# Expert weights fetched as 16 KB runs into eight rotating slots, with permuted features, in a two-block transformer kernel

## The chip, the cores and the metric

The kernel runs on one core of a Trainium2 chip. The metric is the device time in microseconds (us) of one execution; lower is better.

## The reference, cut to what matters

The reference is a transformer: a first block (attention and a gated recurrence, then a layer of 16 experts), two further blocks with dense feed-forward layers, and a final norm. All tensors are float32, 256 tokens of 1,024 features. The change lies in the layer of experts, in which each expert takes the 32 tokens (`cap`) that like it most:

```python
def expert_choice_moe(h, w_router, w_gate, w_up, w_down):
    B, S, D = h.shape                                   # 1, 256, 1024
    cap = max(1, CAPACITY_FACTOR * S // N_EXPERTS)      # 32
    logits = jnp.einsum('bsd,de->bse', h, w_router).astype(jnp.float32)
    aff = jax.nn.softmax(logits, axis=-1)
    gate, idx = lax.top_k(aff.transpose(0, 2, 1), cap)
    xin = jax.vmap(lambda hb, ib: hb[ib])(h, idx)
    hid = jax.nn.silu(jnp.einsum('becd,edf->becf', xin, w_gate)) * jnp.einsum('becd,edf->becf', xin, w_up)
    y = jnp.einsum('becf,efd->becd', hid, w_down) * gate[..., None].astype(h.dtype)
    return jnp.zeros_like(h).at[bidx, idx].add(y)
```

Each of the 16 experts has three matrices of 1,024 x 1,024 float32, 4 MiB each, so the layer reads 201.3 MB. Every weight is used once.

## The kernel before

The program is one block with a stream for each engine, ordered by semaphores. The queue of SP issues all weight loads. ACT and DVE take results out of PSUM, and PE has eight PSUM banks (`bank(b)`, 512 float32 in each partition). Banks 0 to 3 hold the residual sum for the whole layer of experts; banks 4 to 7 are for the experts' own products.

**Loads.** `half` (L426 to L430) fetches 512 columns of all 1,024 rows of one matrix, 2 MiB. Row k*128+p goes to partition p, so a partition gets eight runs of 2 KB (512 float32). There are six places in `ring` (`slot(0)` to `slot(5)`: the two column halves of gate, of up and of down) and two more in `odd_slot`, which take the first halves of gate and of up for every other expert. `loads` waits on the semaphores `used0`, `used1` and `used2` (products of gate, up and down done) and issues the next loads in a fixed order. For the first expert two halves of gate are fetched early, half of up when the first block's weights are done with, and five more halves after `acc_done`.

**PE, one expert** (`expert`, in a loop of eight turns with two experts each):

1. `gather` (L800): 16 products of the normed tokens `xn` with a one-hot matrix `hot_next` put this expert's tokens, features on partitions, into bank 4. DVE scales them by the norm's weight into `xin` (L1686).
2. `quarter` (L811), four times: gate columns 0 to 511 into bank 4, up columns 0 to 511 into bank 5, then the other halves into the same two banks. A quarter has eight products with 32 stationary columns; four of them (`j`) write four groups of 32 partitions of the bank at once, and each group sums a part of the features. Since both halves use one bank, a second half waits until the first has been copied out (`g4_done`, `u4_done`).
3. Two transposes (L829) of `hot_e`, the one-hot matrix weighted by the affinity, for the way back.
4. Fold (L844): 16 products with `fold` add the four partition groups and put hidden features on partitions, into banks 6 and 7 (gate and up of a column half in one bank). ACT applies silu (L1210) and DVE multiplies (L1702), half by half, into `hidT`. PE waits for both halves.
5. Two quarters for down (L811) into banks 5 and 4, copied out by DVE and ACT (L1705, L1212).
6. Four products (L854) with `back` add the result to banks 0 to 3. The last of them count `half_done` and `stage_done`; when these have counted all 16 experts the dense layers start with the update and norm of ACT and DVE.

A product is shown in the trace as two MATMUL records (float32 goes through PE in two passes), so a quarter is x16.

**After the experts.** The memory of `ring` is used again: `raw_sb`, `wh_sb`, `wl_sb`, `xTh_sb`, `xTl_sb`, `hidh_sb` and `hidl_sb` lie in it, in this order. The first weights of the dense layers are fetched once `used0` says that the last expert's gate is done (POOL passes this on as `raw_free`).

Of the kernel before, what the change touches and what calls it, by code (L numbers as in the profile page):

```python
# [15 lines left out]
P = 128  # L16
# [123 lines left out]
def two_blocks(nc, x_in, w_in, w_out, wg, wu, wd, relb, f1g, f1u, f1d, w_in2, w_out2, f2g, f2u, f2d,  # L140
               const, band, onehot, future, one, prm_in, fin_w, out):
    with ExitStack() as ctx:
# [45 lines left out]
        def slot(s, n=512):  # L188
            return ring[:, s * SLOT:s * SLOT + KD * n].rearrange("p (k n) -> p k n", k=KD)

# [16 lines left out]
        n_ss, n_eps, n_std, n_rstd, hold = st(3), st(1), st(TT), st(TT), st(6)  # L207
# [46 lines left out]
        hot = t2(TT * (NE + 1) * CAP).rearrange("p (t e c) -> p t e c", t=TT, e=NE + 1)  # L254
# [5 lines left out]
        affT, topw, chosen, place, ones_e = [t2(S)[0:NE, :] for _ in range(5)]  # L260
# [8 lines left out]
        odd_slot = [t2(SLOT).rearrange("p (k n) -> p k n", k=KD) for _ in range(2)]  # L269
# [55 lines left out]
        def pf(name, i=None):  # L325
# [4 lines left out]
        names = """x_in0 x_in1 const_in one_in band_in mask_in w1_in0 w1_in1 w1_hi w1_lo ex_in0 ex_in1 ex_in2 ex_in3 ex_in4 ex_in5 odd_in0 odd_in1  # L330
            mxT_ps k_scaled late_in tb_out tb_in raw_in0 raw_in1 raw_in2 fin_out
            half_done sq_done ss_ready std_ready rstd_ready diag_dve diag_act xn_dve xn_act xnT_ps xT_act xT_dve acc_done x_act x_dve
            z_ready z_hq z_hf z_hb z_q z_k z_v z_hi z_hg
            lb_max lb_exp lb_done gate_sg gate_lf lev_sub lev_exp lev_q lev_k lev_ps lev_put
            qk_sq qk_ms qk_std qkT_ps qT_done kT_done
            sc_ps sc_nm sc_exp sc_cnt eT_ps eT_act eT_dve o_ps o_put ho_ps ho_sq ho_ms ho_std ho_put gs_done
            masks_zero lg_ps lg_nm lg_exp aff_done affT_ps place_done placeT_ps hot_done xin_ps
            xe_ready hote_done used0 used1 used2 back_ps g4_done u4_done back_done sum_ps esil_done ehid_done
# [8 lines left out]
        ex_in = [sem["ex_in0"], sem["ex_in1"], sem["ex_in2"], sem["ex_in3"], sem["ex_in4"], sem["ex_in5"]]  # L347
# [8 lines left out]
        def buf(f, r):  # L356
            return RUNS["ffn", f, r][0]
# [14 lines left out]
        def used_ffn(L, f, r, s):  # L372

            return used[buf(f, r)], 2 * NE + PRODUCTS[buf(f, r)] * L + RUNS["ffn", f, r][2] + s + 1

        def used_mix(L, m):

            return used[buf_mix(m)], 2 * NE + PRODUCTS[buf_mix(m)] * L + RUNS["mix", m][2] + 1
# [19 lines left out]
        def _(sp):  # L398
# [6 lines left out]
            for p in range(W1):  # L405
# [26 lines left out]
            def first_half(row, odd):  # L432
                half(row, wg, 0, odd_slot[0] if odd else slot(0), sem["odd_in0"] if odd else ex_in[0])
                half(row, wu, 0, odd_slot[1] if odd else slot(2), sem["odd_in1"] if odd else ex_in[2])

            REST = [(1, wg, 1), (3, wu, 1), (5, wd, 1), (4, wd, 0)]
# [3 lines left out]
            half(0, wg, 0, slot(0), ex_in[0])  # L440
            sp.wait_ge(sem["lev_put"], NLEV + 1)
            half(0, wg, 1, slot(1), ex_in[1])
# [8 lines left out]
            half(0, wu, 0, slot(2), ex_in[2])  # L451
            sp.wait_ge(sem["acc_done"], 1)
            for i, w, c in REST[1:]:
                half(0, w, c, slot(i), ex_in[i])
            first_half(D, True)
# [3 lines left out]
            def loads(e, j, downs_last=True):  # L459

                def value(v):
                    return v if isinstance(v, int) else sp.snap(v)

                half_free, free = value(2 * e + 1), value(2 * e + 2)
                row, row_next = value(D * e + D), value(D * e + 2 * D)

# [4 lines left out]
                for r, w in enumerate((wg, wu)):  # L472
                    if downs_last:
                        next_half(r, w)
# [1554 lines left out]
```

## Time and profile before

| | |
|---|---|
| device time, median of 3 runs | 1729.85 us (1727.73 to 1731.01) |
| profiled execution, its span | 1726.3 us |
| PE matmul busy | 1606.1 us, 93% |
| DVE busy, ACT busy | 750.1 us, 663.7 us |
| moved by DMA | 400.12 MB |
| experts, first product to last | 238.8 to 729.5 us |

The profiled execution's own time is its span, 1726.3 us, and what lies before the first and behind the last instruction; the median of the runs shown is 3.5 us above the span. In the profile, PEclk is the granted clock of TensorE as a share of 2.4 GHz (0.5 is 1.2 GHz), DMA is the busy share of the 16 DMA engines, and an arrow (`<-`) names what an engine waited for. PE records are pipelined, so their durations overlap slightly.

### The profile page before, as it was taken

Reading aid. Unit: us, or ns where it says so; the run is one execution under the profiler, and the core shown is the slowest. Engines: PE = TensorE matmul, PEld = TensorE weight load, DVE = VectorE, ACT = ScalarE, POOL = GpSimd, SP = SyncE. Lnnn points to the kernel's source line nnn. Section 1 sums busy time; section 2 is a strip of 40 time slices with the busy share of each in tenths; the row PEclk is TensorE's granted clock in tenths of the full one; section 3 lists DMA queues with packets and bytes.
Section 4 is the critical chain, followed back from the end, with each engine's and each line's share of the span. In section 5 each row is a group of like instructions: output and inputs, shape, how many; then the busy total and the mean of one; then the engine's idle time right before and its main releaser. Section 6 shows DMA issues by size and latency. Waiting matters only on the chain.

```text
span 1726.3 us, 26493 instructions
## 1 busy us (share of the span) xinstructions
PE 1606.1 (93%) x10974; PEld 1299.6 (75%) x10974; DVE 750.1 (43%) x1004; ACT 663.7 (38%) x757; POOL 46.6 (3%) x34
## 2 busy tenths in 40 slices
PE   7996878897888888999999999999999999999998
PEld 7885744443443444499999979999999999889997
DVE  4679531110101101164445765444554447754444
ACT  5564322111111111354345554433634354753343
POOL 0015200000000000000000000000000000000000
PEclk9898979788778878999999999999999999999999
DMA  7522599999999999965555535555465555346552
GB/s 241 178 80 73 198 339 386 387 387 387 387 387 387 387 387 387 369 220 179 185 191 158 163 98 196 193 178 163 152 215 191 174 170 182 115 138 202 193 181 86
DMA packets 249052, 400.12 MB, mean 232 GB/s; under 512 B 4720, under 2 KB 135200, under 8 KB 248864
## 3 DMA queue, kind: packets, MB, share of 16 engines
q1 hardware_dynamic: 247808, 397.74, 66.8%
q10 hardware_dynamic: 1184, 1.57, 0.3%
q8 instruction: 39, 0.64, 0.2%
q14 instruction: 21, 0.17, 0.0%
HBM read 398.23 MB, written 1.06 MB: 231 GB/s over the span
## 4 chain that ended last, share of the span: by engine, by line
PE 65%; SPq 20%; DVE 5%; DMA 4%; issue 3%; ACT 3%; POOL 0%; ACTq 0%; DVEq 0%; POOLq 0%
SPq L430 20%; PE ps L581 12%; PE ps L583 12%; PE ps L582 12%; PE ps L606 6%; PE ps L607 6%; PE ps L608 6%; PE ps L811 4%; DMA ring<-w_in 2%; PE ps L552 2%; PE ps L543 1%; PE ps L800 1%; DMA ring<-w_expert_down 1%; PE ps L844 1%; PE ps L854 1%
## 5 line engine op out<-in xcount | busy, mean ns | idle before, releaser
L1715 DVE TENSOR_TENSOR wl_sb<-raw_sb,wh_sb 128x2048 fp32r<-128x2048 f32 x162 | 370.8, 2292 | 294.1 <-ACT wh_sb L1220 293.8
L581 PE MATMUL ps<-xTh_sb,wh_sb 128*128 128x256 f32 x1696 | 482.2, 284 | 1.0 <-DVE xTl_sb L1410 1.0
L583 PE MATMUL ps<-xTh_sb,wl_sb 128*128 128x256 f32 x1696 | 479.9, 283 | 0.0
L582 PE MATMUL ps<-xTl_sb,wh_sb 128*128 128x256 f32 x1696 | 479.9, 283 | 0.0
L1220 ACT ACTIVATE wh_sb<-raw_sb 128x2048 fp32r<-128x2048 f32 x162 | 309.8, 1915 | 300.0 <-PE ps L583 186.4
L581 PEld LDWEIGHTS ps<-xTh_sb,wh_sb 128*128 128x128 f32 x1696 | 325.3, 192 | 4.5 <-DVE xTl_sb L1410 2.5
L582 PEld LDWEIGHTS ps<-xTl_sb,wh_sb 128*128 128x128 f32 x1696 | 325.4, 192 | 2.2 <-issue 0.7
L583 PEld LDWEIGHTS ps<-xTh_sb,wl_sb 128*128 128x128 f32 x1696 | 325.4, 192 | 0.0
L811 PE MATMUL ps<-ring,work 128*32 128x512 f32 x1280 | 206.0, 791 | 60.8 <-DMA ring<-w_expert_up 38.9
L811 PEld LDWEIGHTS ps<-ring,work 128*32 128x32 f32 x1280 | 45.7, 136 | 182.6 <-issue 153.1
L606 PE MATMUL ps<-wh_sb,hidh_sb 128*128 128x512 f32 x384 | 151.2, 394 | 1.2 <-DVE wl_sb L1715 1.2
L607 PE MATMUL ps<-wl_sb,hidh_sb 128*128 128x512 f32 x384 | 149.9, 390 | 0.0
L608 PE MATMUL ps<-wh_sb,hidl_sb 128*128 128x512 f32 x384 | 149.5, 389 | 0.0
L1698 DVE COPY work<-ps 128x512 f32<-128x512 f32 x32 | 22.1, 692 | 180.5 <-PE ps L811 180.5
L1231 ACT ACTIVATE work<-ps 128x512 f32<-128x512 f32 x44 | 26.5, 603 | 164.0 <-PE ps L583 164.0
L844 PEld LDWEIGHTS ps<-const_sb,work 128*128 128x128 f32 x512 | 70.2, 224 | 19.4 <-issue 19.4
L606 PEld LDWEIGHTS ps<-wh_sb,hidh_sb 128*128 128x128 f32 x384 | 72.3, 188 | 16.2 <-DVE wl_sb L1715 2.0
L608 PEld LDWEIGHTS ps<-wh_sb,hidl_sb 128*128 128x128 f32 x384 | 72.1, 188 | 15.4
L607 PEld LDWEIGHTS ps<-wl_sb,hidh_sb 128*128 128x128 f32 x384 | 72.3, 188 | 13.8 <-issue 0.5
L844 PE MATMUL ps<-const_sb,work 128*128 128x32 f32 x512 | 72.1, 305 | 0.0
L1727 DVE SCALAR_TENSOR_TENSOR work<-work,ps 128x512 f32<-128x512 f32 x44 | 30.4, 690 | 94.0 <-ACT work L1231 94.0
L800 PEld LDWEIGHTS ps<-work,xn_sb 128*128 128x128 f32 x512 | 63.7, 203 | 8.6 <-issue 7.2
(294 smaller groups left out, 1775.2 us busy)
## 6 DMA issues: line engine op xcount, KB each, us to landing
ring<-w_expert_down SPq DMA_DIRECT2D x32, 2048.0 KB, 19.7
ring<-w_expert_gate SPq DMA_DIRECT2D x24, 2048.0 KB, 19.4
ring<-w_expert_up SPq DMA_DIRECT2D x24, 2048.0 KB, 19.8
raw_sb<-ffn_gate SPq DMA_DIRECT2D x44, 1024.0 KB, 5.4
raw_sb<-ffn_up SPq DMA_DIRECT2D x44, 1024.0 KB, 5.3
raw_sb<-ffn_down SPq DMA_DIRECT2D x44, 1024.0 KB, 4.9
raw_sb<-w_in SPq DMA_DIRECT2D x22, 1024.0 KB, 5.4
ring<-w_in SPq DMA_DIRECT2D x16, 1024.0 KB, 5.6
```

What stands on the lines that cost most here:

```text
L430: sp.dma_start(to, rows.rearrange("(k p) n -> p k n", p=P)).then_inc(landed, 16)
L581: pe.matmul(to, w_h[:, k, fs], x_h[:, k, :], start=k == 0, stop=False)
L582: pe.matmul(to, w_h[:, k, fs], x_l[:, k, :], start=False, stop=False)
L583: mm = pe.matmul(to, w_l[:, k, fs], x_h[:, k, :], start=False, stop=k == KD - 1)
L606: pe.matmul(to, left_h[:, k, ts], w_h[:, k, ns], start=False, stop=False, skip_group_check=True)
L607: pe.matmul(to, left_h[:, k, ts], w_l[:, k, ns], start=False, stop=False, skip_group_check=True)
L608: mm = pe.matmul(to, left_l[:, k, ts], w_h[:, k, ns], start=False, stop=last and k == 1, skip_group_check=True)
L800: mm = pe.matmul(bank(4)[:, k * CAP:k * CAP + CAP], xn[:, t, k * P:k * P + P], hot_next[:, t, :], start=t == 0, stop=t == TT - 1)
L811: mm = pe.matmul(bank(b)[j * CAP:j * CAP + CAP, :], stationary[:, Q4 * r + j, :], w[:, Q4 * r + j, :], start=r == 0, stop=r == KD // Q4 - ...
L844: mm = pe.matmul(bank(6 + c)[:, a:a + CAP], src[:, f * P:f * P + P], fold, start=True, stop=True)
L1220: nc.scalar.activation(wh[j], raw[j], ACT.Copy).then_inc(sem["w_hi"], 1)
L1715: dve.tensor_tensor(wl[j], raw[j], wh[j].bitcast(F32), ALU.subtract).then_inc(raw_free[j], 1)
```

## The change

It does five things.

- **Runs.** `half` now takes rows instead of columns: partition p gets rows 8p to 8p+7 of the matrix, of which a half is four whole rows, one run of 16 KB in memory. A partition thus holds features 8p+k and not k*128+p.
- **Features permuted.** To match, `xn` is written permuted (ACT and DVE, `permuted`), the norm's weight is loaded a second time in that order (`norm2p`, a small DMA in the first phase), and `g4` and `u4` are written by ACT and DVE with the features in the order k, q (`"p q k"` read, `"p k q"` written), so that the fold gives hidden features in the order in which down's rows lie.
- **Slots.** Eight slots in rotation: load q (six for each expert) goes to slot q % 8, as soon as the counter `half_used` says that product q-8 is done.
- **Banks.** A half has all 1,024 columns for half of the features, so a matrix's product is two half products, each into two banks: gate and down in banks 4 and 5, up in 6 and 7. `n0_ps` tells that the first bank of the two is complete.
- **Order.** The next expert's gather stands between the fold of gate and that of up. The transposes stand first in an expert, and the back products wait for both copies of the result. PE's loop has four turns with four experts each. Silu is one instruction.

The diff at its core (arguments, names of semaphores and what follows from them left out):

```diff
-        g4, u4, y4 = [[t2(512) for _ in range(2)] for _ in range(3)]
-        e_sil = [t2(4 * CAP) for _ in range(2)]
+        g4, u4 = [t2(FE).rearrange("p (k q) -> p k q", k=KD) for _ in range(2)]
+        y4 = [t2(512) for _ in range(2)]
+        e_sil = t2(KD * CAP)
...
+        slots = [ring[:, s * SLOT:s * SLOT + SLOT] for s in range(6)] + [t2(SLOT) for _ in range(2)]
+        NS = len(slots)
+        def expert_rows(s):
+            return slots[s].rearrange("p (j n) -> p j n", j=Q4)
+        def permuted(a):
+            return a.rearrange("p (k q) -> p q k", k=KD)
...
+                    sp.dma_start(norm2p, bass.AP(one.tensor, a, [[1, KD], [KD * ONE_N, P // KD], [ONE_N, KD]]),
+                                 allow_slow_non_contiguous=True).then_inc(sem["mask_in"], 16)
...
-            def half(row, w, c, to, landed):
-                rows = w.rearrange("e d f -> (e d) f")[bass.ds(row, D), 512 * c:512 * c + 512]
-                sp.dma_start(to, rows.rearrange("(k p) n -> p k n", p=P)).then_inc(landed, 16)
+            def half(i, row, s):
+                rows = (wg, wu, wd)[i // 2].rearrange("e d f -> (e d) f")[bass.ds(row, D), :]
+                lines = rows.rearrange("(p k) n -> p (k n)", p=P)
+                sp.dma_start(slots[s], lines[:, (i % 2) * rows_of:(i % 2 + 1) * rows_of]).then_inc(ex_in[s], 16)
...
+            for i in range(3, 6):
+                half(i, 0, i)
+            for i in range(2):
+                half(i, D, 6 + i)
...
+            def next_half(q, taken, row):
+                sp.wait_ge(sem["half_used"], taken)
+                half(q % 6, row, q % NS)
+            TURN = 4 * 6
+            with sp.Fori(0, (NE * 6 - NS) // TURN) as g:
+                for j in range(TURN):
+                    next_half(NS + j, sp.snap(TURN * g + j + 1), sp.snap(4 * D * g + D * ((NS + j) // 6)))
...
+            def product(b, stationary, q, landed):
+                h, w = q % 2, expert_rows(q % NS)
+                pe.wait_ge(ex_in[q % NS], landed)
+                for n in range(2):
+                    for j in range(Q4):
+                        mm = pe.matmul(bank(b + n)[j * CAP:j * CAP + CAP, :], stationary[:, Q4 * h + j, :],
+                                       w[:, j, 512 * n:512 * n + 512], start=h == 0, stop=h == 1, skip_group_check=True)
+                    if h == 1 and n == 0:
+                        mm.then_inc(sem["n0_ps"], 1)
+                mm.then_inc(sem["half_used"], 1)
...
+                pe.wait_ge(sem["hote_done"], e_th(1, 1))
+                for t in range(TT):
+                    mm = pe.transpose(bank(UP_PS + 1)[:, t * P:t * P + P], hot_e[:, t, :, :].rearrange("p j c -> p (j c)"), ident)
+                mm.then_inc(sem["back_ps"], 1)
+                pe.wait_ge(sem["xe_ready"], e_th(1, 1))
+                product(GATE_PS, xin, q, landed(q))
+                product(GATE_PS, xin, q + 1, landed(q + 1))
+                pe.wait_ge(sem["back_done"], e_th(1, 1))
+                product(UP_PS, xin, q + 2, landed(q + 2))
+                product(UP_PS, xin, q + 3, landed(q + 3))
+                pe.wait_ge(sem["g4_done"], e_th(2, 2))
+                fold_up(g4, GATE_PS, range(KD)).then_inc(sem["fold_ps"], 1)
+                pe.wait_ge(sem["hot_done"], e_th(1, 2))
+                pe.wait_ge(sem["u4_done"], e_th(2, 1))
+                gather()
+                pe.wait_ge(sem["u4_done"], e_th(2, 2))
+                fold_up(u4, GATE_PS + 1, range(Q4)).then_inc(sem["fold_ps"], 1)
+                fold_up(u4, UP_PS + 1, range(Q4, KD)).then_inc(sem["fold_ps"], 1)
+                pe.wait_ge(sem["ehid_done"], e_th(2, 1))
+                product(GATE_PS, hidT, q + 4, landed(q + 4))
+                pe.wait_ge(sem["ehid_done"], e_th(2, 2))
+                product(GATE_PS, hidT, q + 5, landed(q + 5))
+                pe.wait_ge(sem["y4_act"], e_th(1, 1))
+                pe.wait_ge(sem["y4_dve"], e_th(1, 1))
...
-            with pe.Fori(0, NE // 2) as i:
-                expert(i, 0)
-                expert(i, 1)
+            pe.wait_ge(sem["hot_done"], 1)
+            gather()
+            with pe.Fori(0, NE // 4) as g:
+                for i in range(4):
+                    expert(g, i)
...
+                for n in range(2):
+                    act.wait_ge(*((sem["half_used"], 6 * e + 2) if n else (sem["n0_ps"], 3 * e + 1)))
+                    nc.scalar.activation(g4[:, :, 64 * n:64 * n + 64].rearrange("p k q -> p q k"),
+                                         bank(4 + n).rearrange("p (q k) -> p q k", k=KD), ACT.Copy).then_inc(sem["g4_done"], 1)
+                act.wait_ge(sem["fold_ps"], 3 * e + 1)
+                nc.scalar.activation(e_sil, bank(4)[:, 0:KD * CAP], ACT.Silu).then_inc(sem["esil_done"], 1)
...
+            dve.wait_ge(sem["xin_ps"], 1)
+            next_tokens()
+            next_hot(1)
             with dve.Fori(0, NE) as e:
...
+                for n in range(2):
+                    dve.wait_ge(*((sem["half_used"], 6 * e + 4) if n else (sem["n0_ps"], 3 * e + 2)))
+                    dve.tensor_copy(u4[:, :, 64 * n:64 * n + 64].rearrange("p k q -> p q k"),
+                                    bank(6 + n).rearrange("p (q k) -> p q k", k=KD)).then_inc(sem["u4_done"], 1)
+                dve.wait_ge(sem["xin_ps"], e + 2)
+                next_tokens()
+                next_hot(e + 2)
```

## Rows read from the trace of the kernel before

**Rows 1.** The page: the span, PE's clock and DMA in 40 slices.

```profile
span 1726.3 us, 26493 instructions
...
PEclk9898979788778878999999999999999999999999
DMA  7522599999999999965555535555465555346552
GB/s 241 178 80 73 198 339 386 387 387 387 387 387 387 387 387 387 369 220 179 185 191 158 163 98 196 193 178 163 152 215 191 174 170 182 115 138 202 193 181 86
```

**Rows 2.** Windows: us, busy time of each engine, PEclk, DMA share, GB/s.

```profile
300.00:650.00 350.00, 297.52 (x1817) 146.73 (x1817) 37.75 (x95) 55.40 (x84) 0.00 (x0) 0.80 1.05 387
715.00:720.00 5.00, 4.97 (x44) 3.78 (x36) 1.08 (x3) 1.80 (x3) 0.00 (x0) 1.00 1.05 387
720.00:725.00 5.00, 4.34 (x28) 1.09 (x32) 1.01 (x3) 0.28 (x1) 0.00 (x0) 0.66 1.07 365
```

**Rows 3.** Waits of PE from 300 to 650: us in total, times, longest.

```profile
PE ps L811 <- DMA ring<-w_expert_up: 37.0, 11, 4.9
PE ps L811 <- DVE work L1702: 7.6, 11, 0.7
PE ps L811 <- DVE work L1686: 5.6, 10, 0.6
PE ps L811 <- DMA ring<-w_expert_down: 4.6, 3, 2.5
```

**Rows 4.** Timeline of PE, the last expert (no wait for DMA).

```profile
704.54 3.65 PE L800 MATMUL ps<-work,xn_sb 128*128 128x32 f32 x32
708.71 3.64 PE L811 MATMUL ps<-work 128*32 128x512 f32 x32 [0.52 <-DVE work L1686]
712.28 0.44 PE L829 MATMUL ps<-const_sb,work 128*128 128x128 f32 x2
712.64 3.64 PE L811 MATMUL ps<-ring,work 128*32 128x512 f32 x32
716.22 3.76 PE L844 MATMUL ps<-const_sb,work 128*128 128x32 f32 x32
720.66 5.25 PE L811 MATMUL ps<-ring,work 128*32 128x512 f32 x32 [0.69 <-DVE work L1702]
725.85 3.70 PE L854 MATMUL ps<-work 128*128 128x512 f32 x8
```

**Rows 5.** Timeline of PE, groups that ran at the lower clock.

```profile
231.17 7.03 PE L800 MATMUL ps<-work,xn_sb 128*128 128x32 f32 x32 [1.32 <-DVE work L1672]
238.80 5.54 PE L811 MATMUL ps<-ring,work 128*32 128x512 f32 x32 [0.61 <-DVE work L1686]
...
333.60 3.64 PE L811 MATMUL ps<-ring,work 128*32 128x512 f32 x16 [4.67 <-DMA ring<-w_expert_up]
337.17 7.04 PE L844 MATMUL ps<-const_sb,work 128*128 128x32 f32 x32
```

**Rows 6.** Windows, as rows 2, while a load with 12 KB runs is moved.

```profile
25.50:29.00 3.50, 3.50 (x32) 3.50 (x32) 0.00 (x1) 1.96 (x2) 0.00 (x0) 1.00 1.06 440
26.00:28.00 2.00, 2.00 (x19) 2.00 (x18) 0.00 (x0) 0.95 (x1) 0.00 (x0) 1.00 1.03 432
```

**Rows 7.** Timeline of SP's queue around the first expert.

```profile
211.27 3.73 SPq L430 DMA_DIRECT2D ring<-w_expert_down  x2
215.04 5.22 SPq L430 DMA_DIRECT2D work<-w_expert_gate  x1
220.30 5.66 SPq L430 DMA_DIRECT2D work<-w_expert_up  x1
230.82 0.30 SPq L457 DMA_DIRECT2D rel_bias_band<-work  x1
242.69 4.49 SPq L430 DMA_DIRECT2D ring<-w_expert_gate  x2
```

**Rows 8.** Groups by form from 400 to 595: count, busy us, mean ns, idle before.

```profile
L1698 DVE COPY work<-ps 128x512 f32<-128x512 f32 x12 | 8.3, 692 | 77.3 <-PE ps L811 77.3
L1203 ACT ACTIVATE work<-ps 128x512 f32<-128x512 f32 x6 | 3.6, 597 | 53.0 <-PE ps L811 53.0
L1693 DVE TENSOR_SCALAR work<-work 128x128 f32 x12 | 2.8, 279 | 0.0
```

**Rows 9.** Timeline of ACT in the first phase, two pieces of weights.

```profile
58.77 1.92 ACT L1080 ACTIVATE w1h_sb<-ring 128x2048 fp32r<-128x2048 f32 x1 [0.26 <-DMA ring<-w_in]
64.58 1.91 ACT L1080 ACTIVATE w1h_sb<-ring 128x2048 fp32r<-128x2048 f32 x1 [3.89 <-DMA ring<-w_in]
```

**Rows 10.** The page: the queue that fetches PE's code (packets, MB, share).

```profile
q8 instruction: 39, 0.64, 0.2%
```

More of the change, by code:

```diff
@@ L259, in two_blocks @@
         r_mx, r_nm, r_sum, r_rec = t2(TT), t2(TT), t2(TT), t2(TT)
-        affT, topw, chosen, place, ones_e = [t2(S)[0:NE, :] for _ in range(5)]
+        topw, chosen, place, ones_e = [t2(S)[0:NE, :] for _ in range(4)]
         top8 = t2(8)[0:NE, :]
@@ L450, in _ @@
             sp.wait_ge(sem["w1_lo"], W1)
[L451 removed]
+            half(2, 0, 2)
             sp.wait_ge(sem["acc_done"], 1)
[L453 to L455 removed]
+            for i in range(3, 6):
+                half(i, 0, i)
+            for i in range(2):
+                half(i, D, 6 + i)
             sp.wait_ge(sem["tb_rows_done"], 1)
             sp.dma_start(tb_dram.ap(), tb_rows).then_inc(sem["tb_out"], 16)
[L459 to L466, printed above, removed]
[L468 to L482 removed]
@@ L484, in _ @@
-            with sp.Fori(0, NE // 2 - 2) as i:
-                for j in range(2):
-                    loads(sp.snap(2 * i + j), j)
-            loads(NE - 4, 0)
-            loads(NE - 3, 1, downs_last=False)
-            for r, (i, w, c) in enumerate(REST):
-                if r < 3:
-                    sp.wait_ge(used[r], 2 * (NE - 1))
-                half(D * (NE - 1), w, c, slot(i), ex_in[i])
+            def next_half(q, taken, row):
+                sp.wait_ge(sem["half_used"], taken)
+                half(q % 6, row, q % NS)
@@ L799, in gather @@
                     for t in range(TT):
[L800 removed]
+                        mm = pe.matmul(bank(UP_PS)[:, k * CAP:k * CAP + CAP], xn[:, t, k * P:k * P + P], hot_next[:, t, :],
                                        start=t == 0, stop=t == TT - 1)
                 mm.then_inc(sem["xin_ps"], 1)
[L804 to L814 removed]
@@ new lines, in fold_up, with expert, value, landed @@
+            def fold_up(src, b, ks):
+                for i, k in enumerate(ks):
+                    mm = pe.matmul(bank(b)[:, i * CAP:i * CAP + CAP], src[:, k, :], fold, start=True, stop=True)
+                return mm
+            def expert(g, i):
+                def value(per, v):
+                    return pe.snap(per * g + v)
+                def landed(q):
+                    return value(16 * TURN // NS, 16 * (q // NS) + 16)
+                def e_th(per, v):
+                    return value(4 * per, per * i + v)
+                q = 6 * i
+                pe.wait_ge(sem["hote_done"], e_th(1, 1))
[12 more added lines that the diff above has]
+                pe.wait_ge(sem["u4_done"], e_th(2, 1))
+                gather()
+                pe.wait_ge(sem["u4_done"], e_th(2, 2))
[7 more added lines that the diff above has]
+                pe.wait_ge(sem["y4_dve"], e_th(1, 1))
+                for t in range(TT):
+                    for n in range(2):
@@ L1255, in _ @@
                 norm(3 * L + 2, pf("norm0"), XT1 + 14 * L,
-                     between=lambda: hi(buf(0, GATE), nth(L, 0, GATE, 0), (used[0], 2 * NE + PRODUCTS[0] * L)))
+                     between=lambda: hi(buf(0, GATE), nth(L, 0, GATE, 0), (used[0], 1 + PRODUCTS[0] * L)))
                 hi(buf(0, UP), nth(L, 0, UP, 0))
@@ L1957, in _ @@
             pool.memset(ones_e, 1.0).then_inc(sem["masks_zero"], 1)
-            pool.memset(hot[:, :, NE, :], 0.0).then_inc(sem["masks_zero"], 1)
-            pool.wait_ge(sem["used0"], 2 * NE)
+            pool.memset(hot[:, :, NE:NE + 2, :], 0.0).then_inc(sem["masks_zero"], 1)
+            pool.wait_ge(sem["half_used"], 6 * (NE - 1))
             for j in range(3):
                 pool.memset(hold[:, 1 + j:2 + j], 0.0).then_inc(raw_free[j], 1)
+            pool.wait_ge(sem["half_used"], 6 * (NE - 1) + 3)
+            for j in range(3):
+                pool.memset(hold[:, 6 + j:7 + j], 0.0).then_inc(used[j], 1)
             pool.wait_ge(sem["stage_done"], NE)
```

138 lines of the change are left out of this document (38 added, 100 removed).

## The prediction, written before the change was run

> **What bounds the kernel now.** I read the page's 40 slices first [rows 1]. DMA is at the top of its scale for ten slices, from about 259 us, at 387 GB/s, and PEclk is below 9 in most of these; behind them PE is the full engine and DMA is half busy. So the layer of experts is the one stretch that DMA could bound. The window 300 to 650 confirms it: DMA share 1.05 throughout, PE busy 297.5 of 350 us [rows 2]. The waits of PE there say which wait ends last: 41.6 us for expert weights and 13.2 us for two short DVE steps [rows 3]. In this state an expert takes 12.58 MB / 387 GB/s = 32.5 us. The timeline then gives what PE would need by itself: the last expert, with no wait for DMA, takes 704.54 to 729.55, 25.0 us [rows 4]. The whole layer, first product to last, is 238.8 [rows 5] to 729.55 [rows 4], 490.7 us, or 30.7 us an expert: below 32.5, because eight of the 96 halves are there before the first product. DMA is still full at 715 to 720 [rows 2], so the load stream and PE end together. What follows is PE's and is not touched; a gain at 729.55 passes through to the end.
>
> **The rate of DMA.** A half now is one run of 16 KB in each of 128 partitions instead of eight of 2 KB. The trace has no such runs. The nearest is a load in runs of 12 KB: 440 GB/s over 3.5 us and 432 GB/s over 2 us of it [rows 6]. Below, the bound is the rate of today, 387 [rows 2]. I take 430, close under the 12 KB rows, because short windows book a load's edges unevenly. A half of 2.097 MB then takes 4.88 us instead of 5.42, and 88 halves 429.4 us instead of 476.9.
>
> The Trainium skill (DMA: Bandwidth & Descriptors, Why small descriptors are slow) states a fixed overhead of about 3 cycles for each packet, beside one cycle for 32 bytes. By that, runs of 2 KB would lose 4% to it and long runs nearly nothing, so a rate of 1.04 x 387 = 403 GB/s and a stream shorter by 18 us instead of 47. The step from 387 to 440 in rows 2 and 6 is 1.14, so the trace speaks for the larger figure. The same page (Latency and other measured facts, HBM row pitch at large powers of two) speaks against such layouts: rows at pitches of some hundred KB and more in powers of two lost rate. Here partitions lie 32 KB apart, a power of two but well below, and no row of the trace shows such a loss.
>
> **When DMA's stream ends.** Before, the first load behind the prefetched eight is issued at 242.69 [rows 7], when the first product is done; that stream of 88 halves ends at about 242.7 + 1.4 + 476.9 = 721. After the change the first product starts later: DVE now makes the next one-hot matrix and both halves of `hot_e` (279 ns each, [rows 8]) and PE the transposes (0.44, [rows 4]) before it. That is 0.3 + 0.56 + 0.44 = 1.3 us. The five loads behind `acc_done` finish earlier and only lengthen the gap, since no slot is free. So the stream starts at 245.4 and ends at 674.8. Slots don't starve it: PE gives back four in its first 8 us, which keep DMA busy for 19.5 us, and the fifth about 18 us after the start. Behind the last load less is left than it seems: the last expert's fourth half lands at 665.0, then come its product (1.8), fold and gather (7.2 at the full clock), down (3.6), the copy (0.9) and the back products (3.7), 682.2; with the lower clock (next part) about 686.
>
> **When PE's work ends.** The number of products, their shapes and the weight loads are the same. I take the last expert's 25.0 us [rows 4] and change it:
>
> - Removed: the wait for `xin` (0.52) and that for `hidT` (0.69) [rows 4]. The first goes since the gather stands well ahead of its use; the second since the first half of `hidT` is made under the second half of up's fold, and the second under a product. The waits of a second half for the copy of the first go into other banks. 25.0 - 1.2 = 23.8.
> - Freed of the low clock: down took 5.25 where the same 32 records take 3.64 [rows 4]. 22.2 at the full clock.
> - Added: the back products wait for DVE's copy of bank 5, which starts only when the last product ends. 692 ns [rows 8] and two handovers, 0.9. 23.1. Before, DVE's copy lay under the other quarter and PE didn't wait.
> - The copies of gate and up write with a stride. They take 597 and 692 ns now [rows 8]; strided I allow up to twice that. Gate's lie under up's two products (3.64), up's under fold and gather (7.2): no cost. If they took over 3 us, PE would wait.
> - The clock. Fold and gather have 32 columns a product; after a fold and its wait down ran at the lower level (5.25, [rows 4]). Now fold and gather stand together: 64 records, 7.2 us. Below: one fall as today, 1.6. Above: both groups at the lower level (7.04 instead of 3.7, twice, [rows 4, 5]) and both down products too (3.64 for one, [rows 5], instead of 1.8): 6.7 + 3.6 = 10.3. I take one group at the lower level and one fall behind it, 3.3 + 1.7 = 5.0.
>
> So 28.1 us an expert (24.7 to 33.4). PE starts at 240.1, its first products run at the lower clock (5.54 against 3.64, [rows 5]) and 16 experts take 449.6: it ends at 240.1 + 1.9 + 449.6 = 691.6.
>
> **Sum.** DMA allows an end at 686, PE one at 691.6. The two are close, so in some experts PE will still find a half missing; I add 1.5 and expect the last back product at 693 instead of 729.55: 36.5 us earlier. Smaller terms: `norm2p` is 1,024 elements of 4 bytes in SP's queue, ahead of a piece of weights. ACT already waited 0.26 and 3.89 for such pieces [rows 9]; between 0 and 3 us, I take 0.5. The first dense weights may be fetched from the last expert's start and land at about 684, before they are used. Code: below. In total 36.0, on the profiled execution 1726.3 to 1690.3, and as the median of runs 3.5 above the span, 1694.
>
> **Rivals.**
>
> 1. DMA sets the end to the last: the clock falls once an expert as today, PE needs 24.7 and waits for weights. End 684 to 687, time about 1686. For it: waits for DMA dominate now [rows 3]. Against it: the longer run of narrow products. Chance 0.2.
> 2. The rate rises little or not: HBM or the pitch holds it. A quarter of the way from 387 to 440 [rows 2, 6], at 400 GB/s, a half takes 5.24 us, the stream ends at 706.7 and the layer, 11.4 later as above, at 718: time 1719. At 387 it is 722.3 + 11.4 = 733.7, time 1735. The page's rule of 3 cycles (403 GB/s) is this case and gives 1716. For it: no row has 16 KB runs. Against it: [rows 6]. Chance 0.11, of which 0.04 at no gain.
> 3. PE becomes the bound and it is slower than before (the other side). The clock stays low through fold, gather and down, at over 30.4 us an expert ((729.55 - 242.0) / 16 is 30.5) the layer is slower; at 31.5 the end is 746, time 1746. For it: the gather and the fold both took 7.04 at the lower level [rows 5], and PE idles between gate's and up's halves when it is ahead. Against it: a wait of 4.67 was followed by low products, but the loss was paid by time PE had anyway. Chance 0.09, 0.04 of it between 29.5 and 30.4, still faster.
> 4. PE's loop body doubles, from two experts to four, and the code has to be read again in every turn. Code was fetched in 39 packets over the whole run, 0.2% of the 16 engines' span, 1.4 us a packet [rows 10]. If half of that came again and nothing hid it, 20 packets cost 28 us: 1722. Halves that have landed meanwhile hide most of it, since PE then catches up. Chance 0.05. By the Trainium skill (Runtime: NRT & Kernel Launch, Instruction fetch mechanics) PE's instruction memory holds 2,048 instructions, so that such a body would fit; no run here shows its size.
>
> The forecast (PE and DMA close together, 1684 to 1708) has 0.55.
>
> **How the numbers follow.** About 0.2% (3.5 us) is what a measurement tells from no change. Faster: 0.55 + 0.2 + 0.07 (rival 2 at some gain) + 0.04 (rival 3) + 0.03 (rival 4) = 0.89. Same: 0.02. Slower: 0.04 + 0.05 = 0.09. For the range I reach from 1681 (rival 1 at 435 GB/s) to 1720, which takes in 400 GB/s and 29.8 us an expert. Left out: no gain in rate, the slow side of PE and of the code, and a little below.
>
> **What would show it.** In the window 300 to 650: GB/s about 430 at a full share if DMA is still the bound; below 425 with a share under 1.0 says that PE gives slots back too late. PE's waits for expert weights at L811's successor fall from 41.6 us; a wait of 0.7 to 1.0 for DVE's copy appears at each expert's back products. Fold and gather of one expert: 7.2 us says that the clock holds, over 10 that it doesn't. The copies of gate and up: 0.6 to 0.7 us each, or more by their stride. The last back product ends at 693. The prediction is wrong if the rate stays below 410, or if an expert takes PE more than 29.5 us.

## The result, and the profile after

The changed kernel takes 1688.13 us (median of 4 runs, 1686.92 to 1695.01) against 1730.43 us for the kernel before beside it: ratio 0.9771, 95% interval 0.9748 to 0.9794. Forecast were 1694 us and a range of 1681 to 1720. Run again later beside the experiments it took 1692.74 us, ratio 0.9787 (0.9767 to 0.9808).

The page of the changed kernel, the lines that answer to [rows 1]:

```profile
span 1686.5 us, 26658 instructions
...
PEclk9897977878787888999999999999999999999999
DMA  7632479999999999665555436564565546346552
GB/s 233 178 100 76 171 324 428 427 428 428 428 429 428 428 429 429 213 222 176 192 179 165 135 109 218 175 198 150 177 199 174 196 128 213 112 155 194 177 192 80
```

The plateau of the load stream has risen from 387 to 428 GB/s, in ten slices that are each 1.0 us shorter; behind it the clock looks as before and DMA is half busy as before. The windows of the stream and of its start and end (us, busy time of each engine, PEclk, DMA share, GB/s), beside [rows 2]:

```profile
236.00:240.00 4.00, 2.92 (x14) 2.78 (x14) 0.92 (x4) 0.00 (x0) 0.00 (x0) 0.50 0.47 200
...
244.00:246.00 2.00, 2.00 (x24) 0.52 (x20) 0.00 (x0) 1.08 (x2) 0.00 (x0) 1.00 0.45 106
...
300.00:650.00 350.00, 333.01 (x2140) 190.34 (x2132) 52.37 (x113) 75.53 (x88) 0.00 (x0) 0.82 1.01 428
...
675.00:680.00 5.00, 5.00 (x34) 4.39 (x37) 1.10 (x4) 0.00 (x0) 0.00 (x0) 0.71 0.99 364
```

DMA is at its full share in the middle, and PE is busy for 333 of 350 us where it was busy for 297.5. The waits of PE in the same 350 us, beside [rows 3] (us in total, times, longest):

```profile
PE ps L844 <- DVE work L1705: 11.0, 12, 0.9
PE ps L795 <- DMA ring<-w_expert_up: 4.3, 2, 3.0
PE ps L795 <- DMA work<-w_expert_up: 1.6, 1, 1.6
```

Waits for weights fell from 41.6 to 5.9 us. The two DVE waits of before are gone and a new one stands at every expert, 0.92 us for the copy of bank 5. The timeline of PE, one expert without any wait for weights and then the last products of the layer, beside [rows 4]:

```profile
269.33 0.38 PE L820 MATMUL ps<-const_sb,work 128*128 128x128 f32 x2
269.64 3.64 PE L795 MATMUL ps<-work 128*32 128x512 f32 x32
273.10 3.62 PE L795 MATMUL ps<-ring,work 128*32 128x512 f32 x32
276.65 1.97 PE L803 MATMUL ps<-const_sb,work 128*128 128x32 f32 x16
278.45 4.61 PE L783 MATMUL ps<-work,xn_sb 128*128 128x32 f32 x32
282.88 3.60 PE L803 MATMUL ps<-const_sb,work 128*128 128x32 f32 x16
286.41 6.07 PE L795 MATMUL ps<-ring,work 128*32 128x512 f32 x32
293.39 3.67 PE L844 MATMUL ps<-work 128*128 128x512 f32 x8 [0.92 <-DVE work L1705]
...
669.12 1.92 PE L795 MATMUL ps<-ring,work 128*32 128x512 f32 x16 [1.59 <-DMA ring<-w_expert_up]
670.97 1.97 PE L803 MATMUL ps<-const_sb,work 128*128 128x32 f32 x16
672.78 3.74 PE L783 MATMUL ps<-work,xn_sb 128*128 128x32 f32 x32
676.35 2.98 PE L803 MATMUL ps<-const_sb,work 128*128 128x32 f32 x16
679.26 5.91 PE L795 MATMUL ps<-work 128*32 128x512 f32 x32
686.08 3.67 PE L844 MATMUL ps<-work 128*128 128x512 f32 x8 [0.92 <-DVE work L1705]
```

From 269.33 to the next expert's transposes at 296.90 are 27.57 us. The fold of gate takes 1.97 and the fold of up, with as many products, 3.60: the granted clock is 1.00 (2.4 GHz) from 276.65 to 281.0, within the gather it falls to 0.50 (1.2 GHz), and it stays there into down (6.07 instead of 3.64), though PE is busy throughout. The layer's last product ends at 689.75 instead of 729.55, 39.8 us earlier, and the span is shorter by exactly as much (1726.3 to 1686.5).

The last wait for weights of the layer ends at 669.12, when the last expert's fourth half has landed. From there PE works without another one, 20.6 us to the end of the layer. So the end follows the load stream: it is the landing of that half and what PE has to do behind it.

### The profile page after: what moved, and what is told of

Same layout as the page of the kernel before. It is cut to its first block, busy times and chain, and to the rows that moved or that the text cites. A ratio compares the mean times of both kernels' runs of the same rounds, so it can differ in the third digit from the quotient of the medians.

```text
span 1686.5 us, 26658 instructions
## 1 busy us (share of the span) xinstructions
PE 1608.4 (95%) x11006; PEld 1331.8 (79%) x11006; DVE 761.2 (45%) x1006; ACT 676.4 (40%) x741; POOL 46.8 (3%) x37
## 4 chain that ended last, share of the span: by engine, by line
PE 82%; DMA 6%; DVE 6%; ACT 3%; issue 2%; POOL 0%; SPq 0%; DVEq 0%; ACTq 0%; POOLq 0%
PE ps L563 12%; PE ps L565 12%; PE ps L564 12%; PE ps L795 10%; PE ps L588 6%; PE ps L589 6%; PE ps L590 6%; PE ps L783 4%; PE ps L803 4%; DMA ring<-w_expert_up 4%; PE ps L844 3%; DMA ring<-w_in 2%; PE ps L534 1%; PE ps L525 1%; ACT w1h_sb L1073 1%
## 5 line engine op out<-in xcount | busy, mean ns | idle before, releaser
L795 PE MATMUL ps<-ring,work 128*32 128x512 f32 x1152 | 155.7, 693 | 6.0 <-DMA ring<-w_expert_up 5.9
L795 PEld LDWEIGHTS ps<-ring,work 128*32 128x32 f32 x1152 | 38.5, 125 | 103.6 <-issue 92.8
L1693 DVE COPY work<-ps 128x512 f32<-128x512 f32 x32 | 31.2, 1050 | 164.9 <-PE ps L795 164.9
L803 PEld LDWEIGHTS ps<-const_sb,work 128*128 128x128 f32 x512 | 85.5, 260 | 13.4 <-issue 13.4
L1224 ACT ACTIVATE work<-ps 128x512 f32<-128x512 f32 x44 | 26.6, 604 | 164.0 <-PE ps L565 164.0
L1205 ACT ACTIVATE work<-ps 128x512 f32<-128x512 f32 x16 | 9.6, 598 | 200.1 <-PE ps L795 200.1
L803 PE MATMUL ps<-const_sb,work 128*128 128x32 f32 x512 | 88.5, 338 | 0.0
L783 PE MATMUL ps<-work,xn_sb 128*128 128x32 f32 x544 | 85.2, 325 | 1.0 <-DVE work L1666 1.0
L783 PEld LDWEIGHTS ps<-work,xn_sb 128*128 128x128 f32 x544 | 83.4, 245 | 1.1 <-issue 1.1
```

The source lines that it names most:

```text
L783: mm = pe.matmul(bank(UP_PS)[:, k * CAP:k * CAP + CAP], xn[:, t, k * P:k * P + P], hot_next[:, t, :], start=t == 0, stop=t == TT - 1)
L795: mm = pe.matmul(bank(b + n)[j * CAP:j * CAP + CAP, :], stationary[:, Q4 * h + j, :], w[:, j, 512 * n:512 * n + 512], start=h == 0, stop=h ...
L803: mm = pe.matmul(bank(b)[:, i * CAP:i * CAP + CAP], src[:, k, :], fold, start=True, stop=True)
```

## The experiments

Eight edited kernels were run, and the changed kernel once more. The first three separate the length of the runs from all else.

**Runs of 2 KB in the changed kernel.**

```diff
-                lines = rows.rearrange("(p k) n -> p (k n)", p=P)
-                sp.dma_start(slots[s], lines[:, (i % 2) * rows_of:(i % 2 + 1) * rows_of]).then_inc(ex_in[s], 16)
+                lines = rows.rearrange("(p k) (h n) -> p k h n", p=P, h=2)[:, :, i % 2, :]
+                sp.dma_start(slots[s].rearrange("p (k n) -> p k n", n=512), lines).then_inc(ex_in[s], 16)
```

> The changed kernel with everything kept (eight slots, banks, order) but loads in runs of 2 KB: each partition's run is replaced by eight pieces of 512 columns. The weights in the slots are then other ones than the products need, so the output isn't the reference's. My theory, that the length of the runs sets DMA's rate and the rate sets what was gained: 387 GB/s at 300 to 600 us, a stream of 88 halves of 477 us, last back product at about 735 instead of 689.8, time about 1733, no gain over the kernel before. Rival, that slots, banks and order made the gain: time stays at 1688 to 1700.

Measured: 1737.43 us, ratio to before 1.005 (1.0034 to 1.0066). Its window 300 to 600 and its waits of PE from 235 to 720 (the layer ends at 738.5):

```profile
300.00:600.00 300.00, 272.50 (x1622) 152.64 (x1615) 39.63 (x83) 57.36 (x67) 0.00 (x0) 0.76 1.05 387
```

```profile
PE ps L795 <- DMA ring<-w_expert_up: 24.7, 10, 3.5
PE ps L844 <- DVE work L1705: 13.7, 15, 0.9
PE ps L795 <- DMA work<-w_expert_up: 1.7, 1, 1.7
```

The rate is back at 387 and the gain is gone. What is left of the change (slots, banks, order, permuted copies) costs 0.5%. Here neighbouring partitions are loaded from places 32 KB apart and in the kernel before from places 4 KB apart, with runs of 2 KB in both, and the rate is the same 387. So the distance costs nothing here.

**Runs of 4 KB in the changed kernel.** Rows of the two halves alternate, and the products follow.

```diff
-                lines = rows.rearrange("(p k) n -> p (k n)", p=P)
-                sp.dma_start(slots[s], lines[:, (i % 2) * rows_of:(i % 2 + 1) * rows_of]).then_inc(ex_in[s], 16)
+                lines = rows.rearrange("(p k h) n -> p k h n", p=P, h=2)[:, :, i % 2, :]
+                sp.dma_start(expert_rows(s), lines).then_inc(ex_in[s], 16)
...
-                        mm = pe.matmul(bank(b + n)[j * CAP:j * CAP + CAP, :], stationary[:, Q4 * h + j, :],
+                        mm = pe.matmul(bank(b + n)[j * CAP:j * CAP + CAP, :], stationary[:, 2 * j + h, :],
...
-                pe.wait_ge(sem["ehid_done"], e_th(2, 1))
+                pe.wait_ge(sem["ehid_done"], e_th(2, 2))
```

> The changed kernel with loads in runs of 4 KB: a half takes every second row of a partition's eight, and the products take the matching features; down's first half then waits for both parts of hidT. If each run costs a fixed gap besides its bytes, the two rates seen (387 at 2 KB, 428 at 16 KB) give 84.7 and 612.5 ns a run on one of 16 engines, so 9.3 ns a run and 160 ns at 4 KB: 409 GB/s, a stream of 451 us, last back product at about 709, time about 1707. Rival, that only runs well above 4 KB help: 387 to 395 GB/s and 1725 or more; rival, that 4 KB are already enough: 425 and 1690.

Measured: 1710.54 us, ratio 0.9895 (0.9874 to 0.9916), and the last back product ends at 710.81. The window:

```profile
300.00:600.00 300.00, 276.78 (x1758) 156.47 (x1750) 43.19 (x92) 63.06 (x73) 0.00 (x0) 0.81 1.03 409
```

409 GB/s, as a fixed gap of 9.3 ns a run says. Both rivals fall. The single packets of the traces agree: the median packet of 1 KB took 46 ns and one of 12 KB 460 ns (both in the kernel before), one of 2 KB 88, of 4 KB 164, of 16 KB 614, where 9.3 ns and 36.8 ps a byte give 47, 462, 85, 160 and 612.

**Runs of 16 KB in the kernel before.** One place of the source is edited, PE's program stays.

```diff
-                rows = w.rearrange("e d f -> (e d) f")[bass.ds(row, D), 512 * c:512 * c + 512]
-                sp.dma_start(to, rows.rearrange("(k p) n -> p k n", p=P)).then_inc(landed, 16)
+                rows = w.rearrange("e d f -> (e d) f")[bass.ds(row, D), :]
+                lines = rows.rearrange("(p k) n -> p (k n)", p=P)
+                sp.dma_start(to.rearrange("p k n -> p (k n)"), lines[:, SLOT * c:SLOT * c + SLOT]).then_inc(landed, 16)
```

> The kernel before with only the load changed: each half is one run of 16 KB in each partition, the two-expert loop, the slots, the banks and the order stay. The weights in the slots are other ones than the products need, so the output isn't the reference's. If the runs alone make the gain: 428 GB/s, the stream of 88 halves ends at about 674, PE needs 25 to 26 us an expert, last back product at 682 to 690, time 1682 to 1690, the same as the changed kernel or a little below, since its narrow products stand apart and the clock falls less. Rival, that the old fixed order of loads with slots bound to a role can't keep DMA busy at this rate: share under 0.97 and a time of 1700 or more.

Measured: 1686.72 us, ratio 0.9762 (0.9739 to 0.9786). Its window and its waits of PE over the layer:

```profile
300.00:600.00 300.00, 264.58 (x1737) 128.34 (x1740) 36.24 (x92) 53.50 (x82) 0.00 (x0) 0.86 1.01 428
```

```profile
PE ps L812 <- DMA ring<-w_expert_up: 20.5, 11, 3.0
PE ps L812 <- DVE work L1703: 11.0, 16, 0.7
PE ps L812 <- DVE work L1687: 8.9, 16, 0.6
PE ps L812 <- DMA ring<-w_expert_down: 3.0, 2, 1.5
```

The whole gain comes with this edit, and the old order keeps DMA full at 428 GB/s. PE has more room here: 23.5 us of waits for weights against 7.5 in the changed kernel, a mean clock of 0.86 against 0.81 in the same window, and 26.6 us for an expert without such a wait (its gather at 260.11 to the next at 286.75). What this run doesn't show is a kernel with the right output: for that the features have to be permuted, and a half product over all 1,024 columns needs two banks. So slots, banks and order gain no time; that they could all be left out wasn't tried.

The next runs ask what sets the end of the layer now: PE, the stream, or both. The first three of them (split wait, moved gather, norm's weight) ran beside the changed kernel itself:

> The changed kernel once more, unaltered, as the yardstick for the next three on the same chip: 1688.

Measured: 1692.74 us (1687.74 to 1697.32), ratio 0.9787 (0.9767 to 0.9808).

**The wait of the back products split.**

```diff
-                pe.wait_ge(sem["y4_act"], e_th(1, 1))
-                pe.wait_ge(sem["y4_dve"], e_th(1, 1))
                 for t in range(TT):
                     for n in range(2):
+                        if t == 0:
+                            pe.wait_ge(sem["y4_dve"] if n else sem["y4_act"], e_th(1, 1))
```

> The changed kernel with one wait moved: the first back product of an expert waits for ACT's copy alone and only the second for DVE's. The wait of 0.92 us at each expert should shrink to nearly nothing, and an expert of PE from 27.6 to about 26.8 us. If PE sets the end of the layer, 16 x 0.8 = 13 us are gained: 1675. My theory, that PE and the load stream now end together, so that the stream takes over: PE's waits for weights grow by about 12 us, and only the wait behind the last load counts: 1 us, 1687.

Measured: 1688.64 us, ratio 0.9771 (0.9752 to 0.979), not told apart from the control. The waits of PE for weights over the layer:

```profile
PE ps L795 <- DMA ring<-w_expert_up: 13.5, 7, 2.9
PE ps L795 <- DMA work<-w_expert_up: 4.7, 3, 2.6
```

The 14.6 us for DVE's copy are gone, and the waits for weights rose from 7.5 to 18.2. The stream took back 10.7 of the 14.6 us. The layer's first product starts 0.5 us later (241.16) and its last one ends at 689.91, 0.2 us later, so the layer is 0.35 us shorter; the other 3.5 us went into PE's own work, some of it slower (the expert from 640.52 has 3.34, 5.89 and 6.43 where the changed kernel has 1.92, 4.36 and 6.33).

**The gather between the products of down, with the split wait.**

```diff
-                pe.wait_ge(sem["hot_done"], e_th(1, 2))
-                pe.wait_ge(sem["u4_done"], e_th(2, 1))
-                gather()
                 pe.wait_ge(sem["u4_done"], e_th(2, 2))
...
                 product(GATE_PS, hidT, q + 4, landed(q + 4))
+                pe.wait_ge(sem["hot_done"], e_th(1, 2))
+                gather()
                 pe.wait_ge(sem["ehid_done"], e_th(2, 2))
```

(The split wait is as above. DVE's `next_tokens` and `next_hot` move behind the making of `hidT`, with a wait for their own end.)

> As the run with the split wait, and the next expert's gather moved from between the folds to between the two products of down, so that the narrow products stand in two groups of 3.6 us. If the joined group is what the clock falls for, fold and gather take 3.7 each (9.8 together now), and an expert of PE about 25 us or less where no weights are missing. Time: the stream ends at 676 as now; behind it stand a product, the copy and the back products, but the gather of the last expert may now delay the last product. End of the layer 685 to 688, time 1684 to 1687. If PE set the end: 27.6 to 25 is 40 us less, 1648.

Measured: 1690.04 us, ratio 0.977 (0.9757 to 0.9784). Timeline of PE, three products of the first expert, and then one expert without a wait for weights, to the next one's transposes:

```profile
253.05 1.92 PE L795 MATMUL ps<-ring,work 128*32 128x512 f32 x16
254.90 3.76 PE L783 MATMUL ps<-work,xn_sb 128*128 128x32 f32 x32
258.59 1.92 PE L795 MATMUL ps<-ring,work 128*32 128x512 f32 x16
...
290.83 0.38 PE L820 MATMUL ps<-const_sb,work 128*128 128x128 f32 x2
...
298.15 3.76 PE L803 MATMUL ps<-const_sb,work 128*128 128x32 f32 x32
301.84 3.59 PE L795 MATMUL ps<-ring,work 128*32 128x512 f32 x16
305.36 3.95 PE L783 MATMUL ps<-work,xn_sb 128*128 128x32 f32 x32
309.24 3.36 PE L795 MATMUL ps<-ring,work 128*32 128x512 f32 x16
312.53 3.74 PE L843 MATMUL ps<-work 128*128 128x512 f32 x8
316.10 0.38 PE L820 MATMUL ps<-const_sb,work 128*128 128x128 f32 x2
```

The fold and the gather of this expert run at or near the full clock (3.76 and 3.95), but each product of down behind one of them pays (3.59 and 3.36 instead of 1.9; the granted clock is 0.52 and 0.53 there). In the first expert nothing pays: from 249.4 to 260.4 the clock is 1.00. The six experts without a wait for weights take 23.8, 26.8, 25.3, 23.7, 25.3 and 23.8 us (the first from 240.24), 24.8 in the mean instead of 27.6, so PE's part of the expectation came true. The waits for weights grew to 29.0 us in all, and the time stayed: the stream alone sets it. The last product ends at 691.65, since the last expert's gather now stands ahead of its last product of down.

**The norm's weight laid out with the other parameters** (`norm2p` becomes a field of `one_sb`, its DMA goes).

> The changed kernel without the DMA of 1,024 elements of 4 bytes: the norm's weight in the permuted order comes with the other parameters. If that DMA delays the next piece of weights on the path of the first phase: 0.3 to 1 us less, 1687.5. If it is hidden: no difference.

Measured: 1687.52 us (1686.8 to 1690.6), ratio 0.9756 (0.9743 to 0.977). Inconclusive: its interval overlaps the control's, and in its profiled execution the first gather starts at 233.42, not earlier than the 231.91 of the changed kernel and the 231.63 of the control.

**Three small edits together.** The split wait, the norm's weight as above, and:

```diff
-                pe.wait_ge(sem["hote_done"], e_th(1, 1))
-                for t in range(TT):
-                    mm = pe.transpose(bank(UP_PS + 1)[:, t * P:t * P + P], hot_e[:, t, :, :].rearrange("p j c -> p (j c)"), ident)
-                mm.then_inc(sem["back_ps"], 1)
                 pe.wait_ge(sem["xe_ready"], e_th(1, 1))
                 product(GATE_PS, xin, q, landed(q))
+                pe.wait_ge(sem["hote_done"], e_th(1, 1))
+                for t in range(TT):
+                    mm = pe.transpose(bank(UP_PS + 1)[:, t * P:t * P + P], hot_e[:, t, :, :].rearrange("p j c -> p (j c)"), ident)
+                mm.then_inc(sem["back_ps"], 1)
```

> The changed kernel with three small edits: the split wait at the back products, the norm's weight laid out with the other parameters, and the two transposes behind the first product of gate instead of ahead of it. The last lets the first slot of the layer come free 1 to 1.8 us earlier, so the gap of the load stream before the first product shrinks by as much, and the stream sets the end. If so: first load behind the eight issued at 242.5 instead of 244.2, layer 2 us shorter, time 1685 to 1687. If a stretch behind the stream sets the end: no difference from 1688 to 1689.

Measured: 1685.75 us (1684.67 to 1688.47), ratio 0.9752 (0.9739 to 0.9766): the lowest median of all, on another chip than the control. The ratio lies inside the changed kernel's first interval (0.9748 to 0.9794) and just below the control's (0.9767 to 0.9808), so no gain is shown. From the first gather to the first load issued behind the eight it has 11.6 us (229.51 to 241.10), the changed kernel 12.3 (231.91 to 244.24): 0.7 us, less than the 1 to 1.8 expected. The layer isn't the 2 us shorter that were expected either: from the first gather to the last product it takes 458.2 us (229.51 to 687.66), the changed kernel 457.8 (231.91 to 689.75). The lead of the profiled execution is where its first phase happened to end, 2.4 us earlier.

**The gather doubled.**

```diff
-                gather()
+                gather(2)
...
-            def gather():
-                for k in range(KD):
+            def gather(times=1):
+                for k in list(range(KD)) * times:
```

> The changed kernel with one suspected cost doubled: each of the 16 gathers inside the loop is done twice, with the same result, 16 products more an expert. At the full clock they take 3.6 us, at the lower one 7.0. My theory, that PE has almost nothing to spare (27.6 us an expert against 28.1 in which the layer goes by): PE sets the pace at 32 to 34.6 us an expert, the load stream falls below 428 GB/s with a share under 1.0, PE no longer waits for weights, the layer ends at 755 to 795 and the time is 1753 to 1793. Rival, that the stream alone sets the time and PE has several us an expert to spare: under 1720.

Measured: 1817.5 us, ratio 1.0517 (1.0501 to 1.0533), slower than expected. Window, and then the first products behind a turn of the loop and one expert's doubled gather:

```profile
300.00:600.00 300.00, 279.24 (x1647) 176.44 (x1640) 34.02 (x75) 49.61 (x58) 0.00 (x0) 0.74 0.83 341
```

```profile
380.65 0.43 PE L820 MATMUL ps<-const_sb,work 128*128 128x128 f32 x2 [2.72 <-issue]
...
385.60 8.61 PE L795 MATMUL ps<-ring,work 128*32 128x512 f32 x59 [3.52 <-issue]
...
430.35 11.31 PE L783 MATMUL ps<-work,xn_sb 128*128 128x32 f32 x64
```

No wait for weights is left, and DMA is at 0.83. So PE paces the layer, as my theory had it: an expert takes 34.4 us (421.23 to 455.63), and the doubled gather 10.9 to 12.8 us, where the changed kernel's takes 3.7 to 5.9: what was added runs at the lower level, nearly all of it. What I had not expected are the stops marked "issue", in which PE waited for nothing that the profile shows: three pairs, at the three turns back of the loop, 8.5 us ahead of the transposes and 9.9 us within the first product, 18.4 us in all. They are most of the rest of the miss: the first product starts at 239.18, and 239.2 + 1.9 + 16 x 34.4 + 18.4 is 809.9 of the 817.9 at which the layer ends. Of the other 8 us a part stands right behind the stops, where products run at the lower level (8.61 for 59 records where 64 take 7.07 elsewhere): the expert behind the first stop takes 37.1 us besides the stop.

## Why the prediction was right, point by point

The mechanism was right: longer runs raised DMA's rate, and the stream of loads had set the time of the layer. What was wrong is which of the two bounds comes last. The forecast of 693 was PE's path (691.6) and 1.5 for waits; the stream's path was put at 686. In the profile the layer ends with the stream's path, at 689.75, and PE's path by itself would have been done at 683.7. That is the first half of rival 1, DMA sets the end to the last, though not its other half, since PE needs 27.57 us an expert and not 24.7. That the time came within 6 us of the forecast owes something to luck: the two paths lie close together, and one error was up and the other down.

- **DMA's rate.** Forecast 430 GB/s, measured 428. Shown by the runs of 2, 4 and 16 KB (387, 409, 428) to follow from the length of the runs alone, in either kernel. The trace of before had it in the 12 KB rows, better than I read it: the windows of [rows 6] have 440 and 432, but they hold packets of 1 and 1.5 KB too, and the median of 460 ns for the 12 KB packets is 427 GB/s on 16 engines. The Trainium skill's 3 cycles a packet (DMA: Bandwidth & Descriptors, Why small descriptors are slow) would have made 403. The trace doesn't agree: 387 to 428 is 1.106, so the measured gap is 9.3 ns a run, where an estimate by that page's rule is 3.4 (4% of the 84.7 ns of a 2 KB run). The power-of-two pitch (the same page, Latency and other measured facts, where the smallest is 512 KB) cost nothing to be seen at 32 KB: with runs of 2 KB the rate is 387 at a pitch of 32 KB as at 4 KB.
- **Where the stream starts and ends.** Forecast start 245.4; the first load is issued at 244.24, and the window 244 to 246 has a share of 0.45. Forecast landing of the last expert's fourth half 665.0, measured 669.1, so 4 us late. 2.0 us of them are the rate (86 halves take 421.4 us at 428 GB/s and 419.4 at 430), 0.3 us the first issue (forecast 244.0). The rest, near 2 us, I can't divide; the forecast had no term for the time from the last bytes of a half to the semaphore that PE waits for. Behind the landing I had 21 us (665 to 686) and the profile has 20.6.
- **Slots.** Forecast was that they don't starve the stream, and that the fifth comes free about 18 us after the start. The fifth load is issued at 262.45, 18.2 us after the first, and the windows from 248 to 675 have a share of 0.98 or more.
- **PE's expert.** Forecast 28.1, measured 27.57. Term by term: the two removed waits are gone; the wait for DVE's copy is 0.92 (0.9). For the clock I had 5.0, 3.3 in the narrow products and 1.7 behind them. The timeline has 9.76 for folds and gather (276.65 to 286.41) instead of 7.2, and 6.07 for down instead of 3.64: 2.6 and 2.4, so 5.0 too, otherwise divided. What is left at the full clock is 21.6 and not 22.2: each group of the last expert of [rows 4] took a little longer from its start to the next one's, the gather 3.65 and not 3.57, the fold 3.76 and not 3.62, and I had counted its back products to their end (3.70) and not to the next expert's start (3.51).
- **Strided copies.** Allowed up to twice: DVE 1050 ns instead of 692, ACT 1132 instead of 597 [rows 8], and no wait for either. The groups by form, 300 to 600:

```profile
L1200 ACT ACTIVATE work<-ps 128x512 f32<-128x512 f32 x22 | 22.6, 1132 | 25.9 <-PE ps L795 25.9
L1693 DVE COPY work<-ps 128x512 f32<-128x512 f32 x22 | 21.4, 1050 | 110.0 <-PE ps L795 110.0
```

- **The sum.** The last product was forecast at 693 and ended at 689.75. By its own work PE would have been done at 240.65 + 1.9 + 16 x 27.57 = 683.7 (forecast 691.6), and its waits for weights added 7.5 us where I had added 1.5. The two errors, 7.9 down and 6.0 up, nearly cancel.
- **PE and the stream close together.** Right, and tested from both sides: 0.92 us less of PE at each expert, and then 2.8 us less, turned for the most part into waits for weights and gained nothing that the control can resolve; 6.8 us more at each made it 34.4 us an expert, and the layer longer. The layer goes by in 28.07 us an expert (240.65 to 689.75), PE needs 27.57. So the stream has the last word, by a margin of 0.5 us an expert.
- **Code.** Rival 4 was wrong for this kernel but near: see below.
- **What I had not put in the sum.** That slots, banks and order gain nothing of the time: with 16 KB runs the old program of PE does as well, and with 2 KB runs the new one is 0.5% slower. I had argued only that both bounds meet. A part of the 0.5% is the later first load (244.45 against 242.69); how the rest divides wasn't tried. My 0.5 us for the DMA of `norm2p` can't be told from the scatter.

## What to carry to other kernels

When a stream of loads runs at a full DMA share, its GB/s against the length of its runs is the first thing to look at: another load in the same trace with longer runs prices the change before it is made. Then ask what the second bound is and how far away. Here PE was within 2% of it, and behind the stream: edits that freed PE of up to 2.8 us an expert moved waits from one releaser to another and no time, and one that gave it 6.8 us more made it the bound. And when two paths end close together, say which comes last and what stands behind its last wait: here the 20.6 us behind the last landing still count in full, and PE's work elsewhere in the layer nearly not at all. A change that bundles a layout with a new schedule should be split: here one part, the runs, carried all of the gain.

## What the runs showed of the hardware that I had not expected

**The code of a loop.** Queue q8 fetches PE's code. Over the window 260 to 680 it moved, in the changed kernel and then in the one with the doubled gather:

```profile
q8 instruction: 4, 0.07, 0.1%
```

```profile
q8 instruction: 25, 0.41, 0.4%
```

A turn of PE's loop has 1,360 MATMUL and weight load records in the first kernel and 1,616 in the second: an expert has 84 or 100 products with two records of either kind, and two transposes with one of either. The first runs four turns with no stop; the second reads its code again in every turn (9, 9 and 8 packets in the windows 250 to 400, 400 to 540 and 540 to 680) and stops twice at each turn back, 6.1 us a turn in the mean.
**The clock and narrow products.** Products with 32 columns can bring the clock down while PE is busy all the time. A group of 16 of them that starts at the full clock runs at or near it (3.8 to 4.5 us in the run with the moved gather); it was followed by a slow product in some experts (3.59 instead of 1.9 at 301.84 of the run with the moved gather) and not in others (1.92 at 253.05). In a group twice as long, a fold of 8, a gather of 16 and a fold of 8, the last fold is slow nearly always (3.60 instead of 1.97) and the gather in part (3.7 to 5.9). In the one with the doubled gather, the gather takes 10.9 to 12.8 us instead of 7.3. Taking the group apart brought an expert of PE from 27.6 less the 0.92 of the split wait, 26.7, to 23.7 to 26.8, 24.8 in the mean: 1.9 us less in the mean.

**Scatter.** The same kernel's median was 1688.1 and 1692.7 us in two sets of runs. In the profiled executions of all these kernels the first gather starts anywhere from 229.5 to 233.4 us, before anything of the layer of experts has run. And behind the last landing the clock decides: the last expert of the control, the same program, is

```profile
672.40 6.20 PE L783 MATMUL ps<-work,xn_sb 128*128 128x32 f32 x32
678.42 3.60 PE L803 MATMUL ps<-const_sb,work 128*128 128x32 f32 x16
681.95 6.10 PE L795 MATMUL ps<-work 128*32 128x512 f32 x32
688.97 3.67 PE L844 MATMUL ps<-work 128*128 128x512 f32 x8 [0.92 <-DVE work L1705]
```

Its fourth half of weights landed at 668.74, 0.4 us earlier than in the first profile, and its last product ends at 692.64, 2.9 us later: the gather took 6.20 us at a granted clock of 0.58, where the other took 3.74 at 1.00. So differences of 2 to 4 us between these kernels say nothing of the edits.
